# Dilated attention inside a matmul stream: the third pattern's blocks in stops of four

## The reference, cut to what matters

```python
DIL_PATTERNS = ((128, 1), (512, 4), (2048, 16))        # (window, dilation), 4 heads each, BLK = 128
# per pattern: q, k, v go to strided order, in blocks of 128 queries; a block sees
# its own keys and those of the block before it within the same residue
s = q @ k.T * HEAD_DIM ** -0.5; s = where(valid, s, -inf)
m = max(s); e = exp(s - m); l = sum(e); o = (e / l) @ v; lse = m + log(l)
# the three patterns' outputs are weighed by softmax(lse) over the patterns
h = h + concat([pool_out, attn_out]) @ w_out
```

## Time and profile before

| | |
|---|---|
| median of 3 runs | 3148.3 us |
| the profiled execution | 3148.26 us |
| its span, first to last instruction | 3146.5 us |
| PE busy / idle | 3116.4 us / 30.1 us |
| DVE busy | 2038.8 us |
| ACT busy | 978.4 us |
| POOL busy | 1717.0 us |
| mean granted clock of TensorE | 0.998 |

### The profile page before, as it was taken

One profiled execution on the slowest core, in us unless ns is written; L12 is line 12 of the kernel. 1 busy time (PEld: TensorE's weight loads), 2 busy tenths in 40 slices (PEclk: granted clock), 3 DMA queues, 4 the chain that ended last, 5 costly groups with the idle time before them and its releaser, 6 DMA issues.

```text
span 3146.5 us, 39438 instructions
## 1 busy us (share of the span) xinstructions
PE 3116.4 (99%) x14756; PEld 2515.3 (80%) x14756; DVE 2038.8 (65%) x2749; ACT 978.4 (31%) x1847; POOL 1717.0 (55%) x1544
## 2 busy tenths in 40 slices
PE   8999999999999999999999999999999999999999
PEld 6777888888888888777888888888888776788887
DVE  6656576666665765565676666664768988797323
ACT  4222243333332421232343333332432244402112
POOL 5632465666656456532465655655445533476574
PEclk9999999999999999999999999999999999999999
DMA  5111221111112122112131111112111100011112
GB/s 155 50 45 47 75 62 48 54 54 54 49 54 67 51 89 63 40 41 86 48 55 48 53 54 50 53 54 67 46 47 47 34 28 27 21 50 47 51 55 87
DMA packets 306349, 173.73 MB, mean 55 GB/s; under 512 B 61424, under 2 KB 296944, under 8 KB 306160
## 3 DMA queue, kind: packets, MB, share of 16 engines
q1 hardware_dynamic: 287904, 162.55, 17.8%
q10 hardware_dynamic: 18256, 8.67, 0.9%
HBM read 155.13 MB, written 12.91 MB: 53 GB/s over the span
## 4 chain that ended last, share of the span: by engine, by line
PE 94%; DVE 4%; issue 1%; ACT 1%; DMA 0%; ACTq 0%; DVEq 0%; SPq 0%
PE ring L1261 17%; PE ring L1263 17%; PE ring L1262 17%; PE aux L1261 5%; PE aux L1263 5%; PE aux L1262 5%; PE ring L1523 3%; PE ring L1521 3%; PE ring L1522 3%; PE aux L1521 2%; PE aux L1523 2%; PE aux L1522 2%; PE aux L1341 1%; PE aux L1358 1%; PE aux L1628 1%; PE aux L1602 1%
## 5 line engine op out<-in xcount | busy, mean ns | idle before, releaser
L1010 POOL TENSOR_TENSOR w_hi<-w_raw,ones 128x512 fp32r<-128x512 f32 (+3 forms) x408 | 450.1, 1103 | 877.0 <-PE ring L1263 695.1
L1013 POOL TENSOR_TENSOR w_lo<-w_raw,w_hi 128x512 fp32r<-128x512 f32 (+3 forms) x408 | 535.6, 1313 | 32.0
L1261 PE MATMUL ring<-Q_hi,w_hi 128*128 128x512 f32 x1312 | 519.2, 396 | 0.0
L1263 PE MATMUL ring<-Q_hi,w_lo 128*128 128x512 f32 x1312 | 511.2, 390 | 0.0
L1262 PE MATMUL ring<-Q_lo,w_hi 128*128 128x512 f32 x1312 | 511.1, 390 | 0.0
L1261 PEld LDWEIGHTS ring<-Q_hi,w_hi 128*128 128x128 f32 x1312 | 246.2, 188 | 76.6 <-issue 26.3
L1263 PEld LDWEIGHTS ring<-Q_hi,w_lo 128*128 128x128 f32 x1312 | 246.3, 188 | 52.1
L1262 PEld LDWEIGHTS ring<-Q_lo,w_hi 128*128 128x128 f32 x1312 | 246.4, 188 | 50.3 <-issue 1.0
L1261 PE MATMUL ring<-P_hi,w_hi 128*128 128x512 f32 x656 | 270.2, 412 | 3.1 <-DVE pool_u L2291 1.3
L1263 PE MATMUL ring<-P_hi,w_lo 128*128 128x512 f32 x656 | 257.4, 392 | 0.0
L1262 PE MATMUL ring<-P_lo,w_hi 128*128 128x512 f32 x656 | 257.2, 392 | 0.0
(11 more groups left out here) (400 smaller groups left out, 7032.9 us busy)
## 6 DMA issues: line engine op xcount, KB each, us to landing
w_raw<-in_w_in SPq DMA_DIRECT2D x84, 512.0 KB, 3.8
w_raw<-in_w_up SPq DMA_DIRECT2D x64, 512.0 KB, 4.0
w_raw<-in_w_down SPq DMA_DIRECT2D x64, 512.0 KB, 3.4
h_scratch<-h ACTq DMA_DIRECT2D x16, 512.0 KB, 3.6
w_raw<-in_w_gate SPq DMA_DIRECT2D x16, 512.0 KB, 3.9
hx<-h_scratch SPq DMA_DIRECT2D x12, 512.0 KB, 7.6
x_raw<-in_x SPq DMA_DIRECT2D x8, 512.0 KB, 7.7
w_raw<-in_w_out SPq DMA_DIRECT2D x16, 256.0 KB, 2.8
```

What stands on the lines that cost most here:

```text
L1010: g.tensor_tensor(w_hi[:, slot, ks], w_raw[:, slot, ks], one.broadcast_to([P, width, P]), ALU.mult).then_inc(w_hi_ready, 1)
L1013: g.tensor_tensor(w_lo[:, slot, ks], w_raw[:, slot, ks], w_hi[:, slot, ks].bitcast(F32), ALU.subtract).then_inc(w_ready, 1)
L1261: t.matmul(o, wh, xh, start=first, stop=False)
L1263: return t.matmul(o, wl, xh, start=False, stop=last)
```

## The change

Units of the third pattern have two stops of four blocks where they had four stops of two. The number of stops and the blocks of one follow from the unit. The stops of unit 2 are at chunks 11 and 31, (23, 3) and (25, 7); those of unit 5, with the lag, at steps 8, 16, 24 and 32 of part A. Two blocks of a transposed pair lie side by side in one bank, so that DVE copies two blocks in one instruction. Scores of four blocks fill banks 4 and 5, attended blocks all of bank 7. Units of the other patterns keep their stops, but their attended blocks use four places of bank 7 in turn.

```diff
@@ -182,17 +182,44 @@
-STEPS, STOPS, LAG = 8, 4, 2
+STEPS, LAG = 8, 2
+def stops_of(unit):
+    return 2 if unit % GROUPS == 2 else 4
 def unit_parts(unit, i):
-    return ((unit - 1, i + STOPS), (unit, i)) if unit and i < LAG else ((unit, i),)
-def pair_of(i):
-    return 2 * i, 2 * i + 1
+    return ((unit - 1, i + stops_of(unit - 1)), (unit, i)) if unit and i < LAG else ((unit, i),)
+def blocks_of(unit, i):
+    n = STEPS // stops_of(unit)
+    return range(n * i, n * i + n)
+def first_of_stop(unit, j):
+    return j % (STEPS // stops_of(unit)) == 0
+def last_of_stop(unit, j):
+    return j | (STEPS // stops_of(unit) - 1)
+def buffer_of(unit, j):
+    return (j // 2 % 2, j % 2 * P) if stops_of(unit) == 2 else (j % 2, 0)
+def score_at(unit, j):
+    return j % 4 * P if stops_of(unit) == 2 else j % 2 * 256
 def weave():
@@ -215,8 +242,8 @@
         put(m0, 4, "turn_v", unit, 1)
-        for i in range(STOPS):
-            k = 11 + 10 * i
+        for i in range(stops_of(unit)):
+            k = 11 + 40 // stops_of(unit) * i
             put(m0 + k // KC, k % KC, "step", unit, i)
@@ -230,8 +257,8 @@
     put_a(4, "turn_v", 5, 1)
-    for i in range(STOPS + LAG):
-        put_a(8 + 7 * i, "step", 5, i)
+    for i in range(stops_of(5) + LAG):
+        put_a(8 + 8 * i, "step", 5, i)
     put_a(36, "stat_in", 1)
@@ -495,7 +522,7 @@
     read_back = place("read_back", [P, 8, GROUPS, 4], at=at_spare + 2816)
-    neg_max = place("neg_max", [P, 2, 2], at=at_spare + 3200)
+    neg_max = place("neg_max", [P, 4, 2], at=at_spare + 3200)
     top = place("top", [P, 8, 2], at=at_spare + 3232)
@@ -1319,38 +1346,41 @@
         def turn_probs(l, unit, j):
-            g, no = unit % GROUPS, step_no(l, unit, j)
+            g, no, (buf, at) = unit % GROUPS, step_no(l, unit, j), buffer_of(unit, j)
             pe.wait_ge(exped, 2 * no + 2)
-            if no >= 2:
+            if stops_of(unit) == 4 and no >= 2:
                 pe.wait_ge(probs_taken, no - 1)
+            elif first_of_stop(unit, j):
+                pe.wait_ge(probs_taken, no)
             for e in range(2):
                 for b in range(2 if has_prev(g, j) else 1):
-                    mm = t.transpose(turned[j % 2][:, 256 * e + b * P:256 * e + b * P + P], probs[:, j % 2, e, b * P:b * P + P], ident[:])
+                    mm = t.transpose(turned[buf][:, 256 * e + at + b * P:256 * e + at + b * P + P], probs[:, buf, e, at + b * P:at + b * P + P], ident[:])
             mm.then_inc(probs_turned, 1)
         def attend(l, unit, j):
-            g, buf, no, cols = unit % GROUPS, unit % 2, step_no(l, unit, j), slice(j % 2 * P, j % 2 * P + P)
+            g, buf, no, (half, at) = unit % GROUPS, unit % 2, step_no(l, unit, j), buffer_of(unit, j)
+            cols = slice(j % 4 * P, j % 4 * P + P)
             pe.wait_ge(probs_taken, no + 1)
-            if no and j % 2 == 0:
+            if no and first_of_stop(unit, j):
                 pe.wait_ge(attn_taken, no)
...
                     mm = t.matmul(attend_bank[rows, cols], v_t[buf][:, jj, rows],
-                                  probs_t[:, j % 2, e, b * P:b * P + P], start=(b == 0), stop=(b == len(blocks) - 1))
+                                  probs_t[:, half, e, at + b * P:at + b * P + P], start=(b == 0), stop=(b == len(blocks) - 1))
             mm.then_inc(attended, 1)
         def score_block(l, unit, j):
-            g, buf, no, at = unit % GROUPS, unit % 2, step_no(l, unit, j), j % 2 * 256
+            g, buf, no, at = unit % GROUPS, unit % 2, step_no(l, unit, j), score_at(unit, j)
             if j == 0:
...
                     pe.wait_ge(summed, sum_no(l, Y_HN2, 0, 0))
-            if no and j % 2 == 0:
+            if no and first_of_stop(unit, j):
                 pe.wait_ge(masked, 2 * no)
@@ -1362,16 +1392,16 @@
         def attention_stop(l, parts):
             for unit, i in parts:
-                if 1 <= i <= STOPS:
-                    for j in pair_of(i - 1):
+                if 1 <= i <= stops_of(unit):
+                    for j in blocks_of(unit, i - 1):
                         turn_probs(l, unit, j)
...
                 if i >= 2:
-                    for j in pair_of(i - 2):
+                    for j in blocks_of(unit, i - 2):
                         attend(l, unit, j)
             for unit, i in parts:
-                if i < STOPS:
-                    for j in pair_of(i):
+                if i < stops_of(unit):
+                    for j in blocks_of(unit, i):
                         score_block(l, unit, j)
         def mix_channels(l, c, hf):
@@ -1868,8 +1898,8 @@
         def take_attended(l, unit, j):
             c, g = divmod(unit, GROUPS)
-            act.wait_ge(attended, step_no(l, unit, j | 1) + 1)
-            src, dst = attend_bank[:, j % 2 * P:j % 2 * P + P], attn[c][:, g]
+            act.wait_ge(attended, step_no(l, unit, last_of_stop(unit, j)) + 1)
+            src, dst = attend_bank[:, j % 4 * P:j % 4 * P + P], attn[c][:, g]
             if g == 0:
@@ -1880,11 +1910,11 @@
         def exp_block(l, unit, j):
             c, g = divmod(unit, GROUPS)
-            n = 2 * P if has_prev(g, j) else P
+            n, (buf, at) = 2 * P if has_prev(g, j) else P, buffer_of(unit, j)
             act.wait_ge(max_ready, step_no(l, unit, j) + 1)
             for e in range(2):
-                x_ = probs[:, j % 2, e, 0:n]
-                a.activation(x_, x_, ACT.Exp, scale=SCALE, bias=neg_max[:, j % 2, e:e + 1],
+                x_ = probs[:, buf, e, at:at + n]
+                a.activation(x_, x_, ACT.Exp, scale=SCALE, bias=neg_max[:, j % 4, e:e + 1],
                              accum_out=row_stat[:, unit, j, 2 + e:3 + e]).then_inc(exped, 1)
...
@@ -2328,22 +2358,29 @@
         def take_probs(l, unit, j):
...
             no = step_no(l, unit, j)
+            if stops_of(unit) == 2:
+                if j % 2 == 0:
+                    dve.wait_ge(probs_turned, no + 2)
+                    dve.wait_ge(attended, no - (1 if j == 0 else 2))
+                    v.tensor_copy(probs_t[:, j // 2 % 2].rearrange("p e k -> p (e k)"), turned[j // 2 % 2]).then_inc(probs_taken, 2)
+                return
             dve.wait_ge(probs_turned, no + 1)
...
         def take_scores(l, unit, s):
-            g, at = unit % GROUPS, step_no(l, unit, s)
+            g, at, col, (buf, half) = unit % GROUPS, step_no(l, unit, s), score_at(unit, s), buffer_of(unit, s)
             n = 2 * P if has_prev(g, s) else P
...
             dve.wait_ge(attn_consts, l + 1)
-            dve.wait_ge(scored, step_no(l, unit, s | 1) + 1)
+            dve.wait_ge(scored, step_no(l, unit, last_of_stop(unit, s)) + 1)
             for e in range(2):
-                v.tensor_tensor_reduce(out=probs[:, s % 2, e, 0:n], in0=scores[e][:, s % 2 * 256:s % 2 * 256 + n], in1=m, scale=1.0, scalar=-3.0e38,
+                v.tensor_tensor_reduce(out=probs[:, buf, e, half:half + n], in0=scores[e][:, col:col + n], in1=m, scale=1.0, scalar=-3.0e38,
                                        op0=ALU.add, op1=ALU.max, accum_out=row_stat[:, unit, s, e:e + 1]).then_inc(masked, 1)
             dve.wait_ge(masked, 2 * at + 2)
-            v.tensor_scalar(neg_max[:, s % 2], row_stat[:, unit, s, 0:2], -SCALE, None, ALU.mult).then_inc(max_ready, 1)
+            v.tensor_scalar(neg_max[:, s % 4], row_stat[:, unit, s, 0:2], -SCALE, None, ALU.mult).then_inc(max_ready, 1)
         def lower_pool(l, c, hf):
...
```

## The result

The changed kernel takes 3154.09 us (median of 20 runs, 3152.01 to 3156.54) against 3148.64 us (20 runs, 3147.06 to 3150.38): a ratio of 1.0018, 95% interval 1.0011 to 1.0024, which is 5.5 us more. The forecast was 3150.0 us. The profiled execution took 3153.84 us, 5.6 us more than the one of before, so the trace can be read for this difference.

What follows compares the result with a forecast made beforehand. PE was taken to bound the kernel, busy 3116.4 of 3146.5 us. Terms of -3.7 (saving), +4.0 (pool wait) and +1.7 (clock) gave +2.0 us, 3150.3 from 3148.3, said as 3150.0; range 3144.6 to 3154.0 us.

Steps and rivals of the forecast that it cites:

- the clock's term: Behind the longer gaps at pool job L1381, TensorE falls to half clock once more: 1.7 us added.
- The saving, 3.7 us: On PE, 8 merges of stops over two layers save 0.46 us each; bounds 2.4 to 5.0 us.
- The merge of the scores: On PE, sixteen scores in one group instead of two eights save 0.16 us; bounds nothing or twice that.
- The rival in which the merge saves nothing: A group's fixed part on PE returns as a wait inside the longer stop: 3152.3 to 3154.0 us, chance 0.05.
- The wait at the pool job, +4.0 us: Behind unit 2's last score stop, PE waits longer on ACT's exponentials and stores: 3.6 to 4.3 us added over two layers.
- The rival in which the wait is hidden: At the pool jobs, ACT reaches pool_hi in time: 3144.6 us, at best 3143.3, chance 0.2.
- What reads them is not waited for by PE: Both units' row statistics are stored earlier, and PE doesn't wait for their readers: costed at nothing.
- The slower rival: Falls at both L1381 gaps and one at L1395: 3154.7 us with three, 3153.0 with two; chance 0.2.
- a fall shows as triples of 1.2 us behind a gap: Sign on PE's timeline: matmul triples behind a gap take 1.2 us, where 0.69 us is normal.
- The prediction's remark that the rule speaks of longer gaps than any here: The skill's advice against mid-kernel idle gaps concerns longer gaps than this kernel's; as printed it would omit the 1.7 us.

Runs made afterwards that it cites:

- the repetition: The changed kernel run and profiled once more, unedited, beside the kernel before: 3153.78 us, ratio 1.0020.
- unit 2 alone: Against the kernel before, only unit 2 got the longer stops, unit 5 keeping its six stops at the old places: 3153.02 us, ratio 1.0017.

## Why the prediction was wrong

The places and the direction of the terms were right, the time was 4.1 us too low, and the range ended 0.1 us short. The step that failed is the clock's term: one fall at 1.7 us was put in, and two came that cost 4.5 us. By its steps:

- **The saving, 3.7 us: right, slightly low.** It measured 4.1 us in the stretches without a fall. The merge of the scores is worth 2 x 0.65 - 1.09 = 0.21 us and not 0.16, which makes 0.51 us for all four kinds. It can also be read in the changed kernel itself, on PE in layer 0 from unit 5's first stop to the turn of the weights, here behind the same two rows of before:

```profile
319.80 0.38 PE L1328 MATMUL aux<-ident,probs 128*128 128x128 f32 x2
...
355.53 0.60 PE L1387 MATMUL ring<-ident,weights 128*6 128x128 f32 x4
```

```profile
323.36 0.39 PE L1357 MATMUL aux<-ident,probs 128*128 128x128 f32 x2
...
358.51 0.60 PE L1417 MATMUL ring<-ident,weights 128*6 128x128 f32 x4 [0.32 <-DVE weights L2414]
```

  358.51 - 323.36 less 0.32 us of wait is 34.83 us; before it was 355.53 - 319.80 = 35.73 us. Two merges save 0.90 us here, 0.45 each, where 0.46 was said. The rival in which the merge saves nothing falls.
- **The wait at the pool job, +4.0 us: right place and right chain, undersized.** It grew by 5.1 us. The stores were seen as the cause, and moving them gave 3.3 us back. The model took ACT's exponentials as gapless, where one began 0.48 us late behind the long neg_max, and the way from the last exponential's end to pool_hi at 1.45 us, where it was 1.75 in layer 0. The rival in which the wait is hidden falls.
- **"What reads them is not waited for by PE": wrong,** but small. L1417 transposes weights that are made from these statistics, and waits 0.6 us over two layers. Counted from unit 5's first stop, PE reaches it 0.90 us sooner than before (34.83 against 35.73 us), and waits 0.32 us of that: a part of what the stops save isn't kept.
- **The clock, +1.7 us for one fall: the step that failed.** Two falls came, one in each layer, of 2.9 and 1.6 us in the profiled execution, 2.8 and 2.7 us in the repetition. The number was short (one for two) and so was the price: 1.7 us came from a fall behind a gap of 1.9 us, and a gap of 3.6 us cost up to 2.9. That longer gaps had to be priced for themselves was on record in the trace of before, which has one such gap in the middle of PE's stream, with its fall:

```profile
56.41 1.40 PE L1311 MATMUL ring<-sumsq,ones 128*128 128x512 f32 x2 [3.67 <-DVE sumsq L2250]
...
58.89 0.63 PE L1261 MATMUL ring<-P_hi,w_hi 128*128 128x512 f32 x1
...
60.17 0.54 PE L1261 MATMUL ring<-P_hi,w_hi 128*128 128x512 f32 x1
```

  Behind 3.67 us a triple takes 60.17 - 58.89 = 1.28 us, the half clock. The prediction used only the two gaps of 1.9 us, of which one had no fall.

The budget of the profiled executions: -4.1 saved, +5.1 pool wait, +4.5 falls, +0.6 at L1417, which is +6.1 against +5.6 measured. The 0.6 us that PE waited for s_half in before and not here make up the rest, but not as an effect of the change: that wait stood at 118 us, ahead of the first changed stop, and the repetition has one of 0.5 us there. The first 150 us alone differ by up to 3.5 us between profiled executions, so that a fit this close is partly luck.

The slower rival was the right story with its price set too low: it gave 3153.0 us for two falls and asked for a third to reach 3154.7, and two at 2.25 us on average, with the wait 0.8 us longer than its 4.3, came to 3154.1. Its mark, "a fall shows as triples of 1.2 us behind a gap", is what the rows show. It was given 0.2 because 1.9 us "sufficed once" and "failed to once"; that evidence spoke of gaps of 1.9 us, while of the six pool waits of 3.0 to 3.65 us seen here (the changed kernel twice, unit 2 alone once, two layers each) five were followed by a fall. The Trainium skill, "TensorE: Matmul & The Clock Gate", section "Why this matters for your kernels", advises against idle gaps in mid-kernel of more than about 3 us. The forecast's waits, 2.6 to 2.9 us, were just below that, and the measured ones, 3.64 and 3.02 us, are above it: with the wait sized right, the rule would have told against this change. A fall missed one wait of 3.03 us, and others came behind gaps of 1.85 and 1.9 us, of which the rule says nothing; there the measurement decides. The prediction's remark that the rule speaks of longer gaps than any here holds for the attention part alone, as the row of L1311 shows.

## What to carry to other kernels

When work on one engine is gathered into longer pieces, look for what queues behind the last piece, and move that job ahead of the piece first: here this turned a loss of 5.5 us into a gain of 5. Price a gap on TensorE as its length plus what the clock takes behind it, from rows with gaps of the same length, wherever in the trace they stand; here the falls added two thirds to the wait. Read a wait's length from the engine that ends last with its queue counted whole, the issue of its DMAs too. And before the difference of two kernels is put down to one edit, compare their clocks: the two kernels with early pool jobs differ by the stops and by two falls.

## What the runs showed of the hardware

- A fall of the granted clock costs 1.6 or 2.7 to 2.9 us in this stream, and doesn't come every time; what decides was not found: behind 3.03 us none in one execution, behind 3.00 us one of 2.7 us in another, behind 1.85 us one of 1.6 us. Of the 24 waits of 1.9 us at the spread jobs, in twelve profiled executions, 12 were followed by a fall, and the kernel seems to matter: in the two runs of before with early pool jobs all four were, in the three of the changed kernel with them none of six. The reason is open.
- 3.1 us of matmuls whose result nobody reads kept the clock at 1.00 in a wait of 3.8 us, and the kernel took 4.2 us less than with the waits idle.
- Two DMA issues on ACT, 1.23 us on its queue, held up its next instruction: it began 1.75 us behind the last exponential's end, and right behind it once they were moved.
- A 128x2 tensor-scalar on DVE (neg_max) that starts while POOL has a tensor-tensor in work can last until that ends. The one of 0.92 us ran from 200.56 to 201.48 us, and POOL's split, the row below, from 200.17 to 201.45. In the trace of before 28 of the 96 neg_max took over 0.25 us, up to 1.68; each began inside such an instruction of POOL and ended 0.02 to 0.03 us behind it, and none that began outside one took over 0.18 us. One that began over 1 us ahead of POOL's end took 0.17 us all the same, and no run moved POOL's work to test it.

```profile
200.17 1.28 POOL L1040 TENSOR_TENSOR w_lo<-w_raw,w_hi 128x512 fp32r<-128x512 f32 x1
```
